# Other places in SBUF for the weight slots and the activation buffers of a two-stack layer kernel

## The reference

```python
def first_block(x, ...):                  # DEPTH = 2, D_FF = 2816
    for l in range(DEPTH):
        x = x + 0.5 * swiglu(rmsnorm(x, ffn1_norm[l]), ffn1_w_in[l], ffn1_w_out[l])
        x = x + hybrid_mixer(rmsnorm(x, mix_norm[l]), w_in[l], ...)   # delta rule, stick-breaking attention
        x = x + 0.5 * swiglu(rmsnorm(x, ffn2_norm[l]), ffn2_w_in[l], ffn2_w_out[l])

def hybrid_layer(x, ...):                 # second stack, DEPTH = 2, D_FF_2 = 4096
    h = rms_norm(x, g_mix)
    ...                                   # four branches: banded, block-causal, forgetting attention, convolution
    x = x + jnp.sum(gates * proj, axis=2) @ w_o
    hf = rms_norm(x, g_ffn)
    return x + jnp.square(jax.nn.relu(hf @ w_up)) @ w_down
```

## Time and profile before

| | |
|---|---|
| median of 3 runs | 2372.58 us (2372.43 to 2373.84) |
| profiled execution | 2372.5 us, its span 2370.7 us, granted clock 0.994 |
| TensorE matmul busy (PE) | 2327.5 us, 98% of the span, 17022 matmuls |
| TensorE weight load busy (PEld) | 2191.8 us, 92% |
| VectorE, ScalarE, GpSimd busy | 1587.2 us (67%), 1402.8 us (59%), 144.0 us (6%) |
| DMA | 385.60 MB, 163 GB/s in the mean |

### The profile page before, as it was taken

The page is one execution under the profiler, slowest core; times in us unless marked ns, Lnnn a source line. Parts: engine busy times, 40 slices in busy tenths (PEclk is TensorE's granted clock), DMA queues, the critical chain, the costliest instruction groups (busy, mean ns, idle before and its releaser), DMA issues. The chain is left out here.

```text
span 2370.7 us, 40537 instructions
## 1 busy us (share of the span) xinstructions
PE 2327.5 (98%) x17022; PEld 2191.8 (92%) x17022; DVE 1587.2 (67%) x1948; ACT 1402.8 (59%) x1874; POOL 144.0 (6%) x119
## 2 busy tenths in 40 slices
PE   8999999999999999999999999999999999999998
PEld 7999999999999999999999999889999989899997
DVE  5666668856666756667865666659785455978554
ACT  5456788555555545678745555546854454686443
POOL 0000002200000000001300000000040000004000
PEclk9999999999999999999999999999999999999999
DMA  6555444235555555544315556544455555345653
GB/s 229 195 178 179 144 142 143 72 125 178 178 199 175 190 184 188 169 143 141 126 54 177 178 171 202 177 143 125 142 178 193 194 175 163 116 152 180 202 178 124
DMA packets 312452, 385.60 MB, mean 163 GB/s; under 512 B 10812, under 2 KB 287568, under 8 KB 312272
## 3 DMA queue, kind: packets, MB, share of 16 engines
q1 hardware_dynamic: 312160, 382.96, 49.6%
q10 hardware_dynamic: 112, 0.06, 0.0%
HBM read 381.94 MB, written 1.06 MB: 162 GB/s over the span
## 5 line engine op out<-in xcount | busy, mean ns | idle before, releaser
L316 PE MATMUL bank<-xhi,whi 128*128 128x256 f32 x3696 | 1057.2, 286 | 5.0 <-DVE wlo L305 4.1
L318 PE MATMUL bank<-xhi,wlo 128*128 128x256 f32 x3696 | 1044.0, 282 | 0.0
L317 PE MATMUL bank<-xlo,whi 128*128 128x256 f32 x3696 | 1041.4, 282 | 0.0
L294 DVE TENSOR_TENSOR wlo<-raw,whi 128x2048 fp32r<-128x2048 f32 x354 | 815.8, 2306 | 188.8 <-ACT whi L278 183.7
L278 ACT ACTIVATE whi<-raw 128x2048 fp32r<-128x2048 f32 x355 | 675.8, 1905 | 203.3 <-PE bank L318 203.3
L316 PEld LDWEIGHTS bank<-xhi,whi 128*128 128x128 f32 x3696 | 702.4, 190 | 10.3 <-DVE wlo L305 4.2
L317 PEld LDWEIGHTS bank<-xlo,whi 128*128 128x128 f32 x3696 | 700.5, 190 | 5.0 <-issue 1.9
L318 PEld LDWEIGHTS bank<-xhi,wlo 128*128 128x128 f32 x3696 | 700.2, 189 | 0.0
L316 PE MATMUL bank<-whi,yhi 128*128 128x512 f32 x608 | 239.3, 394 | 0.0
L318 PE MATMUL bank<-whi,ylo 128*128 128x512 f32 x608 | 238.3, 392 | 0.0
L317 PE MATMUL bank<-wlo,yhi 128*128 128x512 f32 x608 | 237.2, 390 | 0.0
(11 more groups left out here) (397 smaller groups left out, 2904.4 us busy)
## 6 DMA issues: line engine op xcount, KB each, us to landing
raw<-in_ffn_w_in SPq DMA_DIRECT2D x88, 1024.0 KB, 5.1
raw<-in_w_in SPq DMA_DIRECT2D x88, 1024.0 KB, 5.1
raw<-in_ffn_w_out SPq DMA_DIRECT2D x44, 1024.0 KB, 4.8
raw<-in_w_gate SPq DMA_DIRECT2D x32, 1024.0 KB, 5.6
raw<-in_w_up SPq DMA_DIRECT2D x32, 1024.0 KB, 5.2
raw<-in_w_down SPq DMA_DIRECT2D x32, 1024.0 KB, 4.9
raw<-in_w_branch_b SPq DMA_DIRECT2D x8, 1024.0 KB, 4.8
raw<-in_w_branch_a SPq DMA_DIRECT2D x8, 1024.0 KB, 4.9
```

What stands on the lines that cost most here:

```text
L294: e.tensor_tensor(wlo[s][:, 0:size], raw[s][:, 0:size], whi[s][:, 0:size].bitcast(F32), ALU.subtract)\
L316: e.matmul(o, ahi, bhi, start=start, stop=False, skip_group_check=True)
L317: e.matmul(o, ahi, blo, start=False, stop=False, skip_group_check=True)
L318: return e.matmul(o, alo, bhi, start=False, stop=stop, skip_group_check=True)
```

## The change

Only declarations move. `raw`, `whi` and `wlo` are no longer three lists declared in a row, but nine tensors declared one by one, with the activations and small tensors between them; three Python lists are built from them afterwards. No size, no instruction, no semaphore and no order of work is edited.

```diff
-        raw = [sb(f"raw{s}", [P, room[s]]) for s in range(SLOTS)]
-        whi = [sb(f"whi{s}", [P, room[s]], F32R) for s in range(SLOTS)]
-        wlo = [sb(f"wlo{s}", [P, room[s]], F32R) for s in range(SLOTS)]
-        x = sb("x", [P, TT, D])
+        raw1 = sb("raw1", [P, room[1]])
+        raw2 = sb("raw2", [P, room[2]])
+        pre = [sb(f"pre{i}", [P, 2, T + 3]) for i in range(2)]
...
         xhi = sb("xhi", [P, KC, T], F32R)
         xlo = sb("xlo", [P, KC, T], F32R)
         yhi = sb("yhi", [P, KC, T], F32R)
         ylo = sb("ylo", [P, KC, T], F32R)
+        x = sb("x", [P, TT, D])
+        gate_bias = sb("gate_bias", [P, DEPTH * 32])
+        lnv = sb("lnv", [P, TT])
+        rstd = sb("rstd", [P, TT])
+        whi1 = sb("whi1", [P, room[1]], F32R)
+        whi2 = sb("whi2", [P, room[2]], F32R)
+        wlo1 = sb("wlo1", [P, room[1]], F32R)
+        wlo2 = sb("wlo2", [P, room[2]], F32R)
+        whi0 = sb("whi0", [P, room[0]], F32R)
+        conv_w = sb("conv_w", [P, DEPTH * 96])
+        raw0 = sb("raw0", [P, room[0]])
+        wlo0 = sb("wlo0", [P, room[0]], F32R)
+        later_keys = sb("later_keys", [P, 384])
+        raw, whi, wlo = [raw0, raw1, raw2], [whi0, whi1, whi2], [wlo0, wlo1, wlo2]
         table = sb("table", [P, CONSTANTS.shape[1]])
...
```

More of the change, by code:

```diff
@@ L121, in hybrid_stack_kernel @@
         room = [KC * WIDE_2, UNIT, UNIT]
-        raw = [sb(f"raw{s}", [P, room[s]]) for s in range(SLOTS)]
-        whi = [sb(f"whi{s}", [P, room[s]], F32R) for s in range(SLOTS)]
-        wlo = [sb(f"wlo{s}", [P, room[s]], F32R) for s in range(SLOTS)]
-        x = sb("x", [P, TT, D])
+        raw1 = sb("raw1", [P, room[1]])
+        raw2 = sb("raw2", [P, room[2]])
+        pre = [sb(f"pre{i}", [P, 2, T + 3]) for i in range(2)]
+        const_cols = sb("const_cols", [P, 4])
+        sumsq = sb("sumsq", [P, 4])
+        dt_bias = sb("dt_bias", [P, DEPTH * HEADS])
+        a_log = sb("a_log", [P, DEPTH * HEADS])
+        b_forget = sb("b_forget", [P, DEPTH * 4])
         xhi = sb("xhi", [P, KC, T], F32R)
@@ L136, in hybrid_stack_kernel @@
         ident, ones, le, ge = const("ident"), const("ones"), const("le"), const("ge")
-        const_cols = sb("const_cols", [P, 4])
         eps, one, ln_scale, half_pi = [const_cols[:, i:i + 1] for i in range(4)]
@@ L140, in hybrid_stack_kernel @@
         cols = sb("cols", [P, NV])
[L141 to L146, removed]
         arena = sb("arena", [P, ARENA])
-        gate_bias = sb("gate_bias", [P, DEPTH * 32])
         dw = sb("dw", [P, DEPTH * 62])
-        b_forget = sb("b_forget", [P, DEPTH * 4])
         rotary = sb("rotary", [96, 2 * T])
@@ L164, in hybrid_stack_kernel @@
         conv_rows = arena[0:96, 4352:4608].rearrange("p (l n) -> p l n", l=DEPTH)
-        pre = [sb(f"pre{i}", [P, 2, T + 3]) for i in range(2)]
         small = sb("small", [P, 240])
-        later_keys = sb("later_keys", [P, 384])
         xn = arena[:, 0:TT * D].rearrange("p (t d) -> p t d", t=TT)
```

## The result

| | before | changed |
|---|---|---|
| median | 2372.62 us (2372.43 to 2373.84, 4 runs) | 2336.07 us (2335.61 to 2337.12, 4 runs) |
| ratio | | 0.9848, 95% interval [0.9835, 0.9861] |
| profiled execution, its span | 2372.5, 2370.7 us | 2335.61, 2333.8 us |
| TensorE busy; span less busy | 2327.5, 43.2 us | 2279.8, 54.0 us |

The kernel became faster by 36.6 us; the forecast was 28.2.

A forecast was written before the change was run, and what follows sets the result against it. TensorE's matmul pace was taken as the bound; 22.7 us saved on 256 columns and 5.5 on 512, with 0 for wide units, other engines and waits, took 2372.5 to 2344 us (own range 2330 to 2358, stated range 2300 to 2384).

The forecast's parts named there:

- The bound: Whole kernel: TensorE, busy 98% of the span, sets the time by how fast one matmul follows another.
- The mechanism: In TensorE, next weight load and stream read SBUF together; their start distance modulo 512 bytes (phase) changes the matmul's cost.
- The 256-column term: 12,624 matmuls streaming 256 columns each save 1.8 ns: 22.7 us.
- The wide unit's contrast: 272-column unit, slot 0: chunks at multiples of 128 take 126.7 ns per matmul, at odd multiples of 64 124.2.
- My bounds of 1.0 and 2.5: Lower and upper bound, in ns, of the gain per 256-column matmul.
- the new kind of phase: Products after the change: odd multiples of 64 (feature products 320, row products 192), claimed cheaper than multiples of 128.
- The 512-column term: 2,208 matmuls streaming 512 columns each save 2.5 ns, between bounds 1.0 and 4.7: 5.5 us.
- The waits: TensorE's seven waits behind VectorE grow by at most 0.09 us each; counted as 0.
- No change: Rival, chance 0.14: the load costs TensorE a fixed excess per matmul; time 2368 to 2377 us.
- The breakdown of the excess: Rival, chance 0.12: at a constant good phase far more of the matmuls' excess goes; half of it gives 2279 us.
- the prediction's own signs: Gate and up products per matmul: near 116.8 ns if right, 118 to 119 no change, below 114 breakdown, above 119 slower.
- The slower rival: Chance 0.16: a constant phase keeps load and stream colliding, +1.5 ns on 14,832 matmuls, +22 us, 2395 us.

The follow-up runs named there:

- p384: The changed kernel with the 64-byte tensor dt_bias declared behind the activations instead of ahead, so every phase is 384 instead of 320: 2380.89 us.
- before_pad64: The kernel before with one unused 64-byte tensor ahead of x, so all declared behind wlo stands 64 bytes higher: 2335.26 us.
- p192: The changed kernel with gate_bias declared ahead of the activations and dt_bias and a_log behind them, every phase 192: 2367.34 us.
- p320_moved32: The changed kernel with the 32-byte b_forget declared behind the large buffers; activations and weight slots stand 32 bytes lower, each phase stays 320: 2343.63 us.

## Why the prediction was right, and where it was not

*The bound* was right: TensorE's own pace was the path, and its busy time fell by 47.7 us.

*The mechanism* was right in its main part: the SBUF distance between weight load and stream decides which paces a product can have. p384 (same slots, 64 bytes) and before_pad64 (64 bytes, nothing else) show it; they moved the time by 44.8 us and by 37.4. By the Trainium skill (SBUF — State Buffer, Who interferes with whom) TensorE's two read ports are independent and it waits for no one. By that neither edit could have moved the time. The measurement decides; it shows that the addresses of the two reads matter, not which part of the memory makes them meet.

*The 256-column term was mis-sized.* Predicted -1.8 ns and -22.7 us. Measured over all distances at full clock without a wait: 118.6 to 114.8, -3.8 ns, -47 us on 12,400 matmuls. The wide unit's contrast of 2.5 ns was taken for the price of a phase, paid by each matmul for itself. It does follow the phase, but a unit whose chunks alternate gains nothing in the mean (126.3 ns against 125.4); the gain comes where the phases stay the same and a product settles into the fast pace: 186 products lose 5.3 ns per matmul (186·48·5.3 = 47 us, before the uneven first matmuls of a product are taken off), 65 lose 0.8. My bounds of 1.0 and 2.5 were bounds under the wrong model. That the new kind of phase, the odd multiples of 64, is the cheaper one was only half true: 64 and 320 settle fast, 192 hardly ever (p192).

*The 512-column term* failed: predicted -2.5 ns and -5.5 us, measured 230.0 to 228.8 in the fast pace and 233.3 in the slow one, in the mean 229.9 to 229.6, -0.7 us. The step that failed is that each weight load would pay at least 1.0 ns at a multiple of 128. The trace of before had the answer: the row product of the earlier trace rows, phases 128, 0, 128, ran above the fast pace in its first half alone (56.69 to 59.46, 2.77 us for 12 matmuls, 230.8 ns). From its thirteenth matmul,

```profile
59.46 0.39 PE L316 MATMUL bank<-whi,yhi 128*128 128x512 f32 x1
```

to the next product at 62.21 it took 2.75 us for 12, 229.2 ns: hardly over the fast pace of after. p384 has 128 in every row product and 232.3 ns, so what is dear for one sequence of phases is not so for another.

*The waits*, costed at nothing, took 10.8 us back: span less busy time grew from 43.2 to 54.0. I had allowed 0.09 us for each of seven waits. That entry alone grew by 2.5 us, and most of the rest came at waits of the mixers that I had not counted. My reading, which no run tests: there VectorE's chain runs beside many products, and what they all save arrives at the next wait together.

-47 - 0.7 + 10.8 = -36.9, the difference of the spans. Against -28.2: a gain on 256 columns of twice the size, less a gain on 512 that did not come and a give-back that was not in the sum. That 2336 lies so near the forecast of 2344, and inside its own range of 2330 to 2358, is in part luck: 47 us by itself would have gone beyond that range.

*The rivals.* No change fell. The breakdown of the excess came in part: by the prediction's own signs (116.8 ns if right, under 114 if the excess breaks down) the gate and up products at 113.8 and 113.3 are the breakdown's, on 256 columns and in the fast pace alone. 113.3 ns still has 6.6 over the 106.7 of the columns, and no phase tried went below. By the Trainium skill (TensorE: Matmul & The Clock Gate, Back-to-back issue gap) the formula for single matmuls, which leaves weight loads out, gives an estimate of 109.2 ns for 256 columns. No run here shows it. The slower rival, a constant phase that keeps two reads together, did not happen at 320, but it exists: the uniform phase 384 is 8.2 us slower than the mixed phases of before.

## What to carry to other kernels

Where TensorE is the path and each matmul loads its own weights, measure start to start and compare slots: a difference between identical products in different buffers is a sign that addresses count, and a pad of 64 bytes is the whole experiment. It can go either way: 64 bytes gained the kernel before 37.4 us, and 64 bytes cost the changed kernel 44.8. Look for two sharp values before taking a mean over them; a phase seen in passing prices the passing, not the locked pace. Expect part of a TensorE gain to return as waits behind the engines that work beside it.

## What the runs showed of the hardware that was not expected

- fp32r matmuls of 256 columns with their own weight load have two stable paces at equal phases of 64 or 320 modulo 512: 113.3 and 117.8 ns (at 192 too, but fast in 20 products alone); of 512 columns 228.8 and 233.3. The step is 4.5 ns in both.
- A product keeps the pace that it is handed, over twelve products and 68 us, while nothing comes between. Which pace follows a break or a row product stays open: behind a row product it was always the fast one in the changed kernel, and in p320_moved32 in 37 of 64. The same program had 65 slow products in one execution and 49 in another.
- With the phases 320, 448, 320 (and 64, 192, 64) all products but a handful reach the fast pace, in a block within the first nine matmuls; with one phase at a multiple of 128 (320, 384, 320) not one of 254 did.
- What in the memory has a period of 256 bytes, and what the remaining 6.6 ns are, stays open; uniform phases 0, 128, 256 and 448 were not tried.
